# A decoder trunk in fp32: gates ahead of evacuation, an entry list spread over experts, fewer rank products, bias tables on row halves, plain transposes in attention

## What is computed

```python
def hier_moe(h, ln_g, w_gr, b_gr, w_er, b_er, w1, w3, w2):
    xf = rms_norm(h, ln_g).reshape(n, c)
    grp_w, grp = lax.top_k(softmax(xf @ w_gr + b_gr), 1)           # 4 groups
    ew, ei = lax.top_k(softmax(el[grp]), MOE_TOPK)                  # 2 of 8 experts in it
    weight = grp_w * ew / jnp.sum(ew, -1, keepdims=True)
    expert = grp * MOE_EXPERTS_PER_GROUP + ei                       # 32 experts
    ...                                                             # tokens sorted by expert
    yb = (jax.nn.silu(xb @ w1[e]) * (xb @ w3[e])) @ w2[e]           # hidden 512
    y = jnp.zeros((n, c), yb.dtype).at[buf_t].add(yb * buf_w[:, None])

def nsa_attention(...):                                             # 16 heads of 64, 4 key groups
    oc = masked_softmax(q @ k_cmp + bias) @ v_cmp                   # 31 compressed keys
    o_sel = masked_softmax(q @ k_sel + bias) @ v_sel                # 8 of 8 blocks: causal
    ow = masked_softmax(q @ k_win + bias) @ v_win                   # window 512: causal
    return (g0 * oc + g1 * o_sel + g2 * ow) @ w_o                   # bias: T5 buckets of distance
```

## Time and profile before

| | before |
|---|---|
| median of the runs | 2137.17 us |
| lowest, highest | 2134.55, 2152.69 us |
| profiled execution | 2140.77 us |
| its span, granted clock | 2138.9 us, 0.947 |
| PE busy | 1886.7 us, 88% |
| DVE busy | 587.8 us, 27% |
| ScalarE busy | 360.0 us, 17% |
| GpSimd busy | 131.6 us, 6% |
| DMA | 503.47 MB, mean 235 GB/s |

### The profile page before, as it was taken

How to read it: one execution, slowest core, us unless ns; L and a number is a source line. 1 busy time by engine, 2 the same in 40 slices (tenths; PEclk the granted TensorE clock), 3 DMA queues, 4 the chain that set the end, 5 groups by cost and what they waited for, 6 DMA issues and landing times.

```text
span 2138.9 us, 26574 instructions
## 1 busy us (share of the span) xinstructions
PE 1886.7 (88%) x11422; PEld 1034.7 (48%) x11422; DVE 587.8 (27%) x1258; ACT 360.0 (17%) x839; POOL 131.6 (6%) x200
## 2 busy tenths in 40 slices
PE   6989989897898999899979988999979989988982
PEld 3333357746444444444535576666554444444440
DVE  4454953443111010110120434443231011011003
ACT  3521023311000000000030114553100000000001
POOL 1052010000000000000100002221000000000001
PEclk9998899997999999999879988999979999999996
DMA  4113073235899999999567020000379999999973
GB/s 193 73 54 104 0 172 77 100 145 236 334 406 399 403 394 401 408 402 394 199 192 108 0 99 21 21 21 2 132 305 384 400 402 406 399 402 400 402 288 138
DMA packets 64540, 503.47 MB, mean 235 GB/s; under 512 B 26980, under 2 KB 27364, under 8 KB 45990
## 3 DMA queue, kind: packets, MB, share of 16 engines
q1 hardware_dynamic: 51878, 476.58, 58.0%
q10 hardware_dynamic: 10240, 16.79, 2.2%
q0 software_dynamic: 2304, 8.39, 1.1%
HBM read 465.01 MB, written 36.72 MB: 235 GB/s over the span
## 4 chain that ended last, share of the span: by engine, by line
PE 86%; DVE 9%; issue 3%; ACT 2%; DMA 1%; POOL 0%; SPq 0%; ACTq 0%; POOLq 0%; DVEq 0%; PEldq 0%
PE bank L1292 75%; PE bank L1344 5%; PE bank L1859 2%; PE bank L1675 1%; DVE arena L1147 1%; DVE arena L1142 1%; DVE arena L1276 1%; DVE arena L1173 1%; PE bank L1300 1%; ACT arena L525 0%; PE bank L1853 0%; DVE arena L959 0%; PE bank L1452 0%; DMA arena<-x 0%; DMA arena<-y_rows,ints 0%
## 5 line engine op out<-in xcount | busy, mean ns | idle before, releaser
L1292 PE MATMUL bank<-arena 128*64 128x512 f32 (+10 forms) x5842 | 1341.5, 513 | 56.8 <-DVE arena L1147 33.1
L1292 PEld LDWEIGHTS bank<-arena 128*64 128x64 f32 (+5 forms) x5842 | 581.5, 163 | 748.4 <-issue 680.2
L1081 DVE TENSOR_TENSOR arena<-bank,vec 128x512 f32<-128x512 f32 x64 | 44.3, 692 | 844.5 <-PE bank L1292 844.5
L1292 PEld LDWEIGHTS bank<-const,arena 128*128 128x128 f32 x2048 | 241.2, 197 | 58.5 <-issue 47.1
L1292 PE MATMUL bank<-const,arena 128*128 128x128 f32 x2048 | 253.0, 284 | 9.4 <-DVE const L1074 9.4
L704 ACT ACTIVATE arena<-bank 128x512 f32<-128x512 f32 x64 | 38.2, 597 | 577.0 <-PE bank L1292 577.0
L700 ACT ACTIVATE arena<-bank 128x256 f32<-128x256 f32 x64 | 24.5, 383 | 436.6 <-PE bank L1292 436.6
L500 POOL DMA_INDIRECT arena<-y_rows,ints x16 | 16.0, 999 | 1321.0 <-DMA y_rows<-arena 688.9
L1675 PE MATMUL bank<-const,arena 128*128 128x128 f32 x128 | 28.0, 300 | 70.4 <-DVE arena L1142 70.4
L1344 PE MATMUL bank<-arena 128*64 128x64 f32 (+2 forms) x1760 | 62.8, 225 | 11.5 <-DVE arena L959 4.6
L785 ACT ACTIVATE arena<-arena,small 128x128 f32<-128x128 f32 (+3 forms) x128 | 70.1, 552 | 2.1 <-DVE small L1261 2.1
(11 more groups left out here) (225 smaller groups left out, 933.2 us busy)
## 6 DMA issues: line engine op xcount, KB each, us to landing
arena<-m_w SPq DMA_DIRECT2D x64, 4096.0 KB, 14.4
arena<-m_w SPq DMA_DIRECT2D x64, 2048.0 KB, 10.7
y_rows<-arena ACTq DMA_DIRECT2D x128, 128.0 KB, 8.4
y_rows<-arena SPq DMA_DIRECT2D x2, 3840.0 KB, 31.7
arena<-kv_w SPq DMA_DIRECT2D x1, 6144.0 KB, 17.2
rev_bias<-arena SPq DMA_DIRECT2D x1, 5120.0 KB, 68.9
arena<-b_wqg SPq DMA_DIRECT2D x1, 4288.0 KB, 14.3
arena<-a_wk SPq DMA_DIRECT2D x2, 2048.0 KB, 14.7
```

Source lines behind the costliest of these rows:

```text
L1081: nc.vector.tensor_tensor(xgT[:, n % 2, 4 * q:4 * q + 4, :], bank[2 + q][:, :].rearrange("p (k t) -> p k t", k=4), spread(gain[:, 4 * q:4 ...
L1292: return nc.tensor.matmul(dst, lhsT, rhs, start=start, stop=stop)
```

## The change

Five edits, in the kernel's own order.

1. In `moe_dve` the gate (waits for silu) stands ahead of `x_out`, and `pick_tokens` moves behind `x_out` in odd experts, one pair earlier than it is needed. `place_of` is formed first of the three readings of bank 5, and two picks are made ahead of the experts.
2. The entry list moves from ahead of the experts behind the copies of experts 1 (`count_blocks`), 2 and 3 (`pick_entry`) and 4 (`entries`).
3. The rank products are 5 instead of 14, one over 128 columns and four over 128, 96, 64 and 32.
4. `fwd`, `rev` and `rel` are kept twice, on partitions 0 to 32 and 64 to 96, and the small products alternate between the two; ScalarE evacuates even and odd columns apart.
5. `diag` is gone. GpSimd scales the probabilities in place (`shared` counts each half unit), and PE turns them with transposes, half i=0 ahead of the outputs, half i=1 behind them.

```diff
@@ sync: tables
-            sp.dma_start(fwd, d["bucket_fwd"]).then_inc(sem("bias_in"), 16)
...
+            for i in range(2):
+                sp.dma_start(fwd[i], d["bucket_fwd"]).then_inc(sem("bias_in"), 16)
...
@@ gpsimd: attention
-                if n >= 4:
-                    pool.wait_ge(sem("probs_mm"), at("probs_mm", 2 * (n - 3)))
                 for i in range(2):
                     g = 3 * (2 * m + i) + 1 + b
-                    last = nc.gpsimd.tensor_scalar(diag[:, n % 4, i, :], ident, share[:, n % 4, i:i + 1],
-                                                   gates[:, j, g:g + 1], ALU.mult, ALU.mult)
-                last.then_inc(sem("diag_ready"), 1)
+                    row = probs[:, n % 4, i, 0:P * (j + 1)]
+                    nc.gpsimd.tensor_scalar(row, row, share[:, n % 4, i:i + 1], gates[:, j, g:g + 1], ALU.mult,
+                                            ALU.mult).then_inc(sem("shared"), 1)
@@ vector: experts
                 for e in range(E):
                     n = E * l + e
-                    if e < E - 2:
-                        if e % 2 == 0:
-                            pick_tokens(n // 2 + 1)
-                        x_out(n // 2 + 1, e % 2)
                     dve.wait_ge(sem("silu"), at("silu", n + 1))
                     nc.vector.tensor_tensor(gated[:, n % 2, :], gated[:, n % 2, :], bank[4 + n % 2][:, 256:512],
                                             ALU.mult).then_inc(sem("gated_ready"), 1)
+                    if e < E - 2:
+                        x_out(n // 2 + 1, e % 2)
+                    if e % 2 and e < E - 3:
+                        pick_tokens(n // 2 + 2)
                     dve.wait_ge(sem("gated_T"), at("gated_T", n + 1))
...
+                    if e == 1:
+                        count_blocks()
+                    elif e == 2:
+                        pick_entry(0, hot1)
+                    elif e == 3:
+                        pick_entry(1, hot2)
+                    elif e == 4:
+                        entries()
@@ tensor: ranks
-                for j in range(NJ + 1):
-                    for q in range(min(j + 1, NJ)):
-                        last = mm(bank[5][:, 32 * j:32 * j + 32], cst("before") if q == j else cst("ones"),
-                                  two_hot[:, q, :], q == 0, q == min(j, NJ - 1))
+                nc.tensor.matmul(bank[5][:, 0:128], cst("before"), two_hot.rearrange("p j n -> p (j n)"), start=True,
+                                 stop=False, skip_group_check=True)
+                for q in range(NJ):
+                    last = nc.tensor.matmul(bank[5][:, 32 * q + 32:160].rearrange("p (j n) -> p j n", n=32), cst("ones"),
+                                            spread(two_hot[:, q, :], 1, NJ - q), start=False, stop=q == NJ - 1,
+                                            skip_group_check=True)
@@ tensor: tables
-                mm(bank[m // 32][:, 16 * (m % 32):16 * (m % 32) + 16], fwd[:, 864 - 16 * m:992 - 16 * m], rel)
+                mm(bank[m % 2][:, 16 * (m // 2):16 * (m // 2) + 16], fwd[m % 2][:, 864 - 16 * m:992 - 16 * m], rel[m % 2])
@@ tensor: attention
+            def turned_probs(n, i):
+                m, j, b = UNITS[n]
+                pe.wait_ge(sem("shared"), at("shared", 2 * n + i + 1))
+                if n:
+                    evacuated = "pT_dve" if i else "pT_act"
+                    pe.wait_ge(sem(evacuated), at(evacuated, n))
+                for s in range(j + 1):
+                    last = nc.tensor.transpose(bank[4 + i][:, P * s:P * s + P], probs[:, n % 4, i, P * s:P * s + P], ident)
+                last.then_inc(sem("probs_mm"), 1)
...
                     scores(n)
+                n = tick - 3
+                if 0 <= n < NU:
+                    turned_probs(n, 0)
                 n = tick - 4
                 if n >= 0:
...
+                    outputs(n)
                 n = tick - 3
                 if 0 <= n < NU:
...
+                    turned_probs(n, 1)
```

141 lines of the change are left out of this document (68 added, 73 removed).

## The result

The changed kernel takes 2031.11 us (median of 4 runs, 2027.05 to 2044.52). The kernel before takes 2140.70 beside it (4 runs with those shown). The ratio is 0.9492, with a 95% interval of 0.9449 to 0.9535: 109.6 us less. Forecast were 2041, 96 less than the 2137.17 shown then. The profiled execution took 2029.74 us; its span, 2027.8, is 111.1 less than that of the profiled one of before.

What follows compares the result with a forecast made beforehand. TensorE, 86% of the chain of work that ended last, was taken as the bound. Savings of 40 + 17.6 + 8 + 30 = 95.6 us from 2140.8 gave 2045.2, or 2041 on the median's scale; range 2020 to 2066.

Steps and rivals of the forecast that it cites:

- Gates ahead of evacuation: Experts: gate runs under the gather, saving 0.95 us per even and 0.35 per odd expert, 40 us in two layers.
- Will the weights follow: Experts: weights land 14.6 us after issue, needed after 40.1, leaving 25.5 us, so the weight stream does not stop TensorE.
- Ranks: Start of each expert stage: 18 fewer TensorE instructions and later copies save 4.3 us, less 0.4 for low clock, per layer.
- The stall: Before each layer's second gather: 3.3 us idle behind the entry list goes whole, and 1.6 of low clock comes back.
- Bias tables: Before the next norm: products side by side on two row halves take about 11.7 us, not 23.3; 8 us saved.
- Attention: Attention: turning by transposes in a new order saves 3.6 us per pair of heads, 30 us; bounds 18 to 42.
- GpSimd: Attention: scaling a 512-column row takes 1.0 us, four widths 2.9, 11.6 a pair of heads, hidden under TensorE's 20.9.
- Attention paid: Rival in attention: GpSimd or the coupling of four engines replaces TensorE, whole 30 us lost, 2071; chance 8%.
- DMA didn't hold the experts: Rival in the experts: DMA holds them at their old period, 40 us lost, 2081; chance 3%.
- the half rows ran side by side: Rival in the bias tables: products on half rows do not run side by side, 8 us lost, 2049; chance 8%.
- Attention at 1.2 GHz: Rival in attention: transposes lose the full clock, 88 us more there, kernel at 2159, slower by 1.0%; chance 3%.

## Why the prediction was right, and where it missed

- **Gates ahead of evacuation: 40 forecast, 40.3 measured.** The step held to the hundredth: starts on DVE 0.61 and 0.60 apart, PE going on at 723.35 after a gather that ended at 722.24, periods of 15.40 and 16.00. Undone it costs 40.7, and the 0.60 that the pick was said to cost in odd experts came back (16.8 of 16.8 us) when it moved.
- **Will the weights follow: yes, and the slack argument was right in size.** It had 25.5 us of lead; in the changed kernel weights land about 25 to 26 us before their products begin. At 14.44 us per expert the lead began at 23.1 and was gone 24 experts later. The assumption that DMA might do no better than 16.36 per expert was pessimistic: it can do about 15.35.
- **Ranks: 4.3 - 0.4 a layer forecast, 3.5 to 3.8 measured**, and 3.2 to 3.7 when the products alone are undone, all with the scatter named above. Nearer to the place, from the first rank product to `place_of`, it is 4.15 less, forecast 4.3. The wider products nearly kept the pace: 10 instructions in 2.34 us, 0.23 each.
- **The stall: 4.9 a layer forecast, 5.0 measured**, 3.3 of waiting and 1.6 of low clock as worked out. The prediction said that it goes "whole, since two picks are made before the experts"; the experiment with the list ahead shows that this clause was enough for four fifths of it. The rest, 1 us a layer, is the list's place ahead of the first gate, which the prediction did not name.
- **Bias tables: 8 forecast, 7.6 measured**, with two small errors against each other. From the last silu to the first scaling it is 34.2 us in before and 34.1 with the tables on one half, and 25.3 to 26.7 in the changed kernel and the other experiments (28.3 and 28.9 with the turning inside the gather and all weights, where the last expert is late). So the gain is sure, 7.5 to 8.9. The tables take 10.0 us and not 11.7. But the second combine started 19.13 us after the last result's start, where it had been 18.07, for its rows came later. The prediction had named it as late next.
- **Attention: 30 forecast, 42.4 measured, at the far end of its bounds.** The mechanism is right (two instructions become one: 80 x 0.112 - 40 x 0.109 = 4.6 us a pair, as forecast). Two terms were mis-sized. First the changes of kind: the prediction priced each at 0.2 and charged 1.6 for eight more. Measured by groups a change to the scores costs 0.21, to a product with the diagonal 0.195, but to transposes or outputs 0.15. So all changes cost 4.4 before and 5.3 after, 0.8 more and not 1.6. Second the waits: they were taken as what was left over after the other terms, 0.6; as the changes had been put at 4.8 where they are 4.4, and the scores with their waiting in before take 8 x 0.918 = 7.3 against 5.9 without, the waits were 1.4. The compressed branch gave 0.1. Together 4.6 - 0.8 + 1.4 + 0.1 = 5.3, measured 5.27. A remainder of a sum carries the errors of all its terms; the wait could have been read from the starts of the score groups.
- **GpSimd: hidden, as forecast.** The row of 512 columns took 0.77 us and not 1.0, the four widths 2.45 and not 2.9. The point from which it decides was put at 5.2; doubled to 4.9, with 0.4 of added waits, it already bound a PE that had become faster than forecast.
- **Rivals.** Attention paid; DMA didn't hold the experts; the half rows ran side by side. Attention at 1.2 GHz did not come: the granted clock of the window above is 1.00, with transposes in every step. The Trainium skill's rule (TensorE: Matmul & The Clock Gate, Part 4: PE-mode transpose) says that the full clock does not engage for transposes, which don't count as busy in the same way. As the prediction's rival applied it, the stage would have grown, and it shrank by a fifth. But products stand between these transposes, so the stage doesn't test transposes alone. For those there is only the earlier trace rows, and it shows less than the prediction took from it: the pace doubled, from 16 in 3.35 us to 17 in 1.70, but the granted clock reads 1.00 over both stretches, so the rise from 1.2 to 2.4 GHz is inferred from the pace and not seen.
- **What no step foresaw** is the 3.0 us of the unchanged first stage.

The version with the turning inside the gather is the fastest: 0.922 of before, about 2.8% under the changed kernel. By its queues it should need both halves, PE's order so that the copy is covered, and VectorE's order so that the copy comes before the evacuation; neither was run alone.

## What to carry to other kernels

Write down, for each engine's queue, what an instruction that can run early is queued behind: a gate behind an evacuation and a pick behind a list were worth 50 us here, and their data had been ready. Then look at what the critical engine can issue while it waits, such as the rest of a gather around two transposes. Before believing that a stream is at its limit, work out its lead and its deficit per step; a busy share near 1 with data still on time is not a limit.

## What the runs showed of the hardware

- DMA engines with a busy share of 0.98 to 1.01 moved 401, 417, 427 and 431 GB/s, as the kernel asked. At 14.44 us per expert the stream fell behind, at 15.40 it held (427 GB/s). The Trainium skill (DMA: Bandwidth & Descriptors, Where 436 GB/s comes from) puts the ceiling of one core's ports at 435 GB/s; the trace agrees, with 431 as its highest long stretch. The same section says that between HBM and SBUF the HBM side binds at about 358; here the weights came from HBM at up to 431, so that bound did not hold for this core.
- A change of kind on PE has a price of its own in attention, by the table of groups: 0.15 us to transposes and to outputs, 0.195 to products with the diagonal, 0.21 to the scores.
- GpSimd's scaling in place of fp32 rows takes 452, 558, 665 and 772 ns for 128, 256, 384 and 512 columns: 0.107 per 128 columns on top of 0.345.
- In unchanged code of the first stage the granted clock of 200 to 250 us had a mean of 1.00 in some executions and 0.66 to 0.69 in others, and the stage ended up to 22 us later. With 1.00 `two_hot` came at 504.9 to 510.6 us; with 0.66 at 526.3 to 527.4; in before and in one experiment, with 0.69, at 511.3 and 513.7. The rows are of the changed kernel and of the one with the gate behind:

```profile
200.00:250.00 50.00, 48.45 (x106) 18.27 (x105) 41.48 (x59) 8.23 (x14) 0.95 (x1) 1.00 0.12 52
```

```profile
200.00:250.00 50.00, 48.75 (x68) 14.87 (x67) 40.02 (x58) 5.84 (x10) 0.95 (x1) 0.66 0.16 69
```

What makes the clock fall there was not tried.
